# Contexts' way through the second block as a program of its own beside x's, all products 256 wide

## What is computed

```python
def first_block(x, ...):                      # two layers, on x only
    for l in range(DEPTH):
        mix = even_mixer(...) if l % 2 == 0 else odd_mixer(...)   # attention and a recurrence; dilated attention
        x = layer_norm(ALPHA * x + mix, ln1_g[l], ln1_b[l])
        hdn = jnp.square(jax.nn.relu(x @ ffn_w1[l]))              # 1024 -> 4096
        x = layer_norm(ALPHA * x + hdn @ ffn_w2[l], ln2_g[l], ln2_b[l])
        x = x + jax.nn.sigmoid(x @ ple_w_gate[l]) * rms_norm(p[l] @ ple_w_proj[l], ple_norm_g[l])
```

## Time and profile before

| what | us |
|---|---|
| three timed runs, median (lowest to highest) | 1990.55 (1989.61 to 1991.17) |
| the profiled execution, device time | 1993.38 |
| its span in the profile | 1992.1 |
| TensorE busy in the span | 1874.0 |
| VectorE busy | 1096.3 |
| ScalarE busy | 885.6 |

### The profile page before, as it was taken

One profiled execution on the slowest core, in us unless ns is written; L12 is line 12 of the kernel. 1 busy time (PEld: TensorE's weight loads), 2 busy tenths in 40 slices (PEclk: granted clock), 3 DMA queues, 4 the chain that ended last, 5 costly groups with the idle time before them and its releaser, 6 DMA issues. The chain is left out here.

```text
span 1992.1 us, 29858 instructions
## 1 busy us (share of the span) xinstructions
PE 1874.0 (94%) x12320; PEld 1583.5 (79%) x12320; DVE 1096.3 (55%) x1971; ACT 885.6 (44%) x1495; POOL 94.2 (5%) x92
## 2 busy tenths in 40 slices
PE   6988999999999999889999989999999799979998
PEld 5956899978868999677775668888888687569998
DVE  5556656566756565646546663333334575555554
ACT  4554545355435453655434442222232664444443
POOL 0000100040001000310101000000000001100000
PEclk9989999999999999898999989999999899989999
DMA  7477655575366555331220022222322222124553
GB/s 267 162 250 267 218 184 184 191 263 202 104 236 230 185 181 183 131 111 46 75 85 22 23 73 95 99 94 94 104 96 96 74 75 85 53 85 161 185 184 107
DMA packets 79624, 276.88 MB, mean 139 GB/s; under 512 B 9200, under 2 KB 13168, under 8 KB 79488
## 3 DMA queue, kind: packets, MB, share of 16 engines
q1 hardware_dynamic: 77840, 269.66, 39.9%
q0 software_dynamic: 1648, 5.31, 0.9%
HBM read 273.88 MB, written 1.05 MB: 138 GB/s over the span
## 5 line engine op out<-in xcount | busy, mean ns | idle before, releaser
L404 DVE TENSOR_TENSOR low<-ring,high 128x1024 fp32r<-128x1024 f32 x410 | 502.4, 1227 | 436.2 <-ACT high L396 434.9
L429 PE MATMUL bank<-XH,high 128*128 128x256 f32 (+1 forms) x2096 | 684.4, 327 | 60.8 <-DVE XL L1511 21.8
L430 PE MATMUL bank<-XL,high 128*128 128x256 f32 (+1 forms) x2096 | 666.0, 318 | 0.0
L431 PE MATMUL bank<-XH,low 128*128 128x256 f32 (+1 forms) x2096 | 665.1, 317 | 0.0
L396 ACT CAST high<-ring 128x1024 fp32r<-128x1024 f32 x410 | 428.1, 1045 | 471.8 <-PE bank L431 418.8
L429 PEld LDWEIGHTS bank<-XH,high 128*128 128x128 f32 x2096 | 406.5, 194 | 117.0 <-DVE XL L1511 27.4
L430 PEld LDWEIGHTS bank<-XL,high 128*128 128x128 f32 x2096 | 407.7, 195 | 23.8 <-issue 0.2
L431 PEld LDWEIGHTS bank<-XH,low 128*128 128x128 f32 x2096 | 407.0, 194 | 24.6
L431 PE MATMUL bank<-hidden_high,low 128*128 128x256 f32 (+1 forms) x864 | 264.6, 306 | 0.0
L430 PE MATMUL bank<-hidden_low,high 128*128 128x256 f32 (+1 forms) x864 | 264.1, 306 | 0.0
L429 PE MATMUL bank<-hidden_high,high 128*128 128x256 f32 (+1 forms) x864 | 261.9, 303 | 0.0
(11 more groups left out here) (304 smaller groups left out, 1934.4 us busy)
## 6 DMA issues: line engine op xcount, KB each, us to landing
ring<-in_stream SPq DMA_DIRECT2D x410, 512.0 KB, 3.2
ring_mod<-in_stream SPq DMA_DIRECT2D x96, 512.0 KB, 5.5
nb<-in_rpb POOLq DMA_DIRECT2D x12, 256.0 KB, 3.2
X<-in_x SPq DMA_DIRECT2D x2, 512.0 KB, 4.0
X<-in_ctx SPq DMA_DIRECT2D x1, 1024.0 KB, 7.4
out<-y SPq DMA_DIRECT2D x8, 128.0 KB, 2.0
pT<-in_p POOLq DMA_DIRECT2D x2, 256.0 KB, 6.3
c_window<-in_window POOLq DMA_DIRECT2D x1, 512.0 KB, 4.3
```

Source lines behind the costliest of these rows:

```text
L404: nc.vector.tensor_tensor(k.low[:, j % SPLIT, :], k.ring[:, j % RING, :], k.high[:, j % SPLIT, :].bitcast(F32), ALU.subtract).then_inc(*V. ...
L429: nc.tensor.matmul(out, wh, xh, start=(i == 0), stop=False)
L430: nc.tensor.matmul(out, wh, xl, start=False, stop=False)
L431: m = nc.tensor.matmul(out, wl, xh, start=False, stop=(c == ks[-1]))
```

## The change

Contexts get a program of their own. `Path("x")` and `Path("c")` each have their own `X`, `XH`, `XL`, squares, roots, temporaries, small rows and slots of banks, and each takes its weights from its own `Stream`. x's is the 410 tiles as before. Contexts' is a second one, `side`, of 110 tiles: 97 for layer 0 and 13 for layer 1's keys, values and states. They are read a second time from where x's copy of them lies in HBM (`TILE_AT`), with two raw slots and two cast slots, and are cast and split anew. Every product with weights stationary is now 256 wide.

Beside that: `low` now shares its memory with the raw ring (five slots, three for `high`), so that a raw slot is free only when TensorE has used the tile, not when VectorE has split it. Banks are 0 and 1 for x's products, 5 to 7 for x's small steps (with 0 and 1 where needed), and 2 to 4 for everything of contexts and the modulations. Attention has two slots of scores instead of three. The swiglu is done in three parts of the width instead of two, and its silu is made from tanh with two steps on VectorE. The function tables of ScalarE are tracked, which gives 30 table loads instead of 43. The copy of x on GpSimd at the end of each first-block layer is gone.

Order is set by a pace: a part of class `Pace` has a rank that depends on how many tiles it has used against a plan over the planner's clock. The modulations' plan is all 96 tiles by 300 us of that clock. Contexts' plan begins at 300 and is 17 tiles by 850 and 110 by 1520. Behind its plan a part has rank -3 (modulations) or -6 (contexts) and goes before everything else; ahead of it, 3 and 5. Contexts start only when all modulations are done.

```diff
-RING = 4
-SPLIT = 4
+RING, SPLIT = 5, 3
+RING_SIDE, SPLIT_SIDE = 2, 2
 RING_MOD = 4
+MAIN_TILES, MOD_TILES = 410, 96
...
+        self.main = Stream(self, "main", RING, SPLIT, None)
+        self.side = Stream(self, "side", RING_SIDE, SPLIT_SIDE, second_tiles("c", 0) + second_tiles("c", 1))
...
-        self.banks = {"gemm": Slots(self, (0, 1)), "bg": Slots(self, (2,)), "small": Slots(self, (3, 4, 5, 6, 7))}
-        self.tmp, self.sq = Slots(self, (0, 1, 2, 3)), Slots(self, (0, 1))
-        self.stream = {"main": [], "mod": []}
-        self.order, self.blocks, self.expected = [], [], {}
+        state = {}
+        x.gemm, x.banks, x.wide = (Slots(self, ids, state) for ids in ((0, 1), (5, 6, 7), (5, 6, 7, 0, 1)))
+        c.gemm = c.banks = c.wide = Slots(self, (2, 3, 4), state)
...
+def tensor_contexts(k):
+
+
+    yield "mod", 1, MOD_PASSES - 1
+    for layer in range(DEPTH):
+        yield from tensor_second(k, k.pc, layer)
...
+def sync_tiles(k, st):
 
     nc, D_ = k.nc, k.D
-    for j in range(k.n_tiles["main"]):
-        if j >= RING:
-            D_.wait_ge(k.s_low_, (yield "low", j - RING))
+    n = MAIN_TILES if st.plan is None else len(st.plan)
+    if st is k.side:
+
+        D_.wait_for((yield "mod used", MOD_TILES - 1))
+    for j in range(n):
+        if j >= st.n_ring:
+            D_.wait_for((yield st.name, "used", j - st.n_ring))
         else:
             yield None
-        nc.sync.dma_start(k.ring[:, j % RING, :], k.io["stream"][len(k.order)]).then_inc(
-            *D_.tick(k.s_raw[j % RING], 0.1, ("raw", j), by=16, later=3.3))
+        at = j if st.plan is None else TILE_AT[st.plan[j]]
+        nc.sync.dma_start(st.ring[:, j % st.n_ring, :], k.io["stream"][at]).then_inc(
+            *D_.tick(st.s_raw[j % st.n_ring], 0.1, (st.name, "raw", j), by=16, later=3.3))
         D_.clock += 1.3
...
+    for j in range(MAIN_TILES if st.plan is None else len(st.plan)):
+        if j >= st.n_split:
+            A.wait_for((yield st.name, "used", j - st.n_split))
+        A.wait_ge(st.s_raw[j % st.n_ring], (yield st.name, "raw", j))
+        nc.scalar.copy(st.high[:, j % st.n_split, :], st.ring[:, j % st.n_ring, :]).then_inc(
+            *A.tick(st.s_high, A_us(TB * P), (st.name, "high", j)))
...
+def vector_low(k, st):
...
+        V.wait_ge(st.s_high, (yield st.name, "high", j))
+        nc.vector.tensor_tensor(st.low[:, j % st.n_ring, :], st.ring[:, j % st.n_ring, :],
+                                st.high[:, j % st.n_split, :].bitcast(F32), ALU.subtract).then_inc(
+            *V.tick(st.s_low, V_us(TB * P), (st.name, "low", j)))
...
+        nc.scalar.activation(w.TMP[:, j, :], k.bank[k.bank_of[tag, "gate", "product", i]][:, 0:SEQ], ACT.Tanh,
+                             scale=0.5).then_inc(*A.tick(k.s_copied, A_us(SEQ), (tag, "tanh", i)))
...
+        t = w.TMP[:, k.tmp_of[tag, i], :]
+        nc.vector.scalar_tensor_tensor(t, t, 1.0, k.bank[k.bank_of[tag, "gate", "product", i]][:, 0:SEQ], ALU.add,
+                                       ALU.mult).then_inc(*V.tick(k.s_vec, V_us(SEQ), (tag, "silu", i)))
...
+        nc.vector.scalar_tensor_tensor(t, t, 0.5, k.bank[k.bank_of[tag, "up", "product", i]][:, 0:SEQ], ALU.mult,
+                                       ALU.mult).then_inc(*V.tick(k.s_vec, V_us(SEQ), (tag, "made", i)))
...
+        now, due = self.k.T.clock, 0.0
+        for (t0, n0), (t1, n1) in zip(self.plan, self.plan[1:]):
+            if now >= t0:
+                due = n0 + (n1 - n0) * min(1.0, (now - t0) / (t1 - t0))
+        return self.late if self.done() < due else self.rank
+
+
+MOD_PLAN = [(0, 0), (300, MOD_TILES)]
+SIDE_PLAN = [(300, 0), (850, 17), (1520, 110)]
...
+    mods = Pace(k, lambda: len(k.mod_blocks) / TB, MOD_PLAN, -3, 3)
+    side = Pace(k, lambda: len(k.side.blocks) / TB, SIDE_PLAN, -6, 5)
+    k.add(T, tensor_modulations(k), mods)
+    k.add(T, tensor_contexts(k), side + 1)
+    k.add(A, scalar_high(k, k.main), split_ahead(k, k.main, -1, 2))
+    k.add(V, vector_low(k, k.main), split_ahead(k, k.main, -1, 2))
+    k.add(A, scalar_high(k, k.side), side)
```

More of the change, by code:

```diff
@@ L1635, in tensor_gla @@
+        for part in range(NQ):
+            T.wait_ge(k.s_copied, (yield ("gla V", w.name, layer), "copied", part))
         T.wait_ge(k.s_act, (yield tag(i), "k turned"))
-        order = list(range(n_chunks)) if d == 0 else [3, 2, 1, 0, 7, 6, 5, 4]
+        order = gla_order(d)
+        steps = order if w.name == "c" else order[:-1]
         banks = []
         for j in range(2):
-            banks.append((yield from k.banks["small"].take(T, (tag(i), "state", n_chunks - 2))))
+            banks.append((yield from w.banks.take(T, (tag(i), "state", len(steps) - 1))))
@@ L2264, in emit @@
+    k.add(V, vector_final(k, x), 0)
     k.add(D_, sync_stores(k), 0)
     k.run()
-    for which, j in k.order:
-        k.blocks += k.stream[which][j * TB:(j + 1) * TB]
-    k.split = k.n_tiles["main"]
-def vector_gains_all(k, jobs):
-    for layer, name, section, tag, after in jobs:
-        for x in after:
-            if isinstance(x, tuple):
-                k.V.wait_for((yield x))
-        first = section // DC
-        yield from vector_gains(k, layer, name, section, tag, range(first, first + 2))
```

1801 lines of the change are left out of this document (952 added, 849 removed).

## The result

The changed kernel took 1997.69 us (median of 9 runs, 1993.22 to 2007.63), the kernel before 1989.61 us (9 runs, 1984.61 to 1992.23). The ratio is 1.0055, 95% interval 1.0037 to 1.0074: **8 us slower** by the medians (11 by the ratio), where 1.6% faster was forecast. The profiled execution took 1999.76 us, with a span of 1998.5.

The account below looks back on a forecast made before the run. TensorE, busy 94%, was taken as the bound. 1993.4 + 31.5 - 70 + 8 + 3 - 4 = 1961.9; with timed runs 2.8 us lower, 1959 us, 1.6% faster. Own range 1942 to 1978; 8 in 10, 1915 to 2015.

Parts of the forecast that it names:

- splitting: Second block's layer 0: 2352 products 512 wide become pairs of 256, each pair 0.0134 us more on TensorE: +31.5 us.
- the start: All 96 modulation tiles come before about main tile 91, leaving early transfers no slack: +8 us, between 0 and +20.
- fewer buffers: x's attention with two score slots, small steps with three banks, and a shorter cast lead: +3 us, 0 to +12.
- filling and layer 1: Side products fill TensorE's gaps, -70 us (bounds -115 and -20); second block's layer 1, -4 us.
- 95 us of loss: TensorE's loss from 400 to 1525 us, taken as the middle of the two bounds; three quarters was to be filled.
- lower bound of 69: Middle stretch's loss as idle time of 46.6 us plus the clock's shortfall of 22.5 us.
- upper of 120: Middle stretch's loss with eight gaps lost end to end (85.9), 11.3 us idle outside them and 22.5 of clock.
- 25 or less as the sign of filling: Idle plus slow clock between main tile 91 and x's layer 1 was to fall from 69 to 25 us or less.
- A second stream at no cost: 110 more tiles fetched, cast and split would make neither VectorE (66%) nor ScalarE the bound: costed at nothing.
- the side tiles come late: Rival: x's products wait behind uncast side tiles, 2018 us, chance 0.22; sign: such waits over 35 us in sum.
- Layer 1: Second block's last stretch: x's recurrence chain is shorter but loses context products as cover: -4 us, -15 to +10.
- Cancel: Rival: two fifths of the loss are filled, so the gain and the split's cost cancel: 1991 us, chance 0.08.

Follow-up runs that it names:

- e2: Kernel before, with every 512-wide product with weights stationary issued as two of 256, each with its own weight load: 2020.8 us, ratio 1.0149.
- e3: Kernel before, with the modulations on the changed kernel's early plan (all 96 tiles by 300 us of the planner's clock): 2013.0 us, ratio 1.0118.
- e4: Kernel before, with the changed kernel's ring: low parts in the raw ring's memory, five raw slots held until used, three high slots: 1982.6 us, ratio 0.9963.
- e5: Changed kernel, with the modulations back in the places they have in the kernel before and contexts' start moved behind them: 1982.9 us, ratio 0.9968.
- c4: c2 with contexts' parts on TensorE held while ahead of their plan, so that they do not fill: 1997.9 us, ratio 1.0041.
- c2: e11 with c1's edit to the pace of contexts' remaining steps: 1981.4 us, ratio 0.9958.
- e8: Changed kernel, with contexts' plan drawn out so that 19 side tiles are left for x's second layer: 2037.6 us, ratio 1.0235.
- c1: Changed kernel, with contexts' remaining steps keeping a late part's rank once all 110 side tiles are used: 1991.4 us, ratio 1.0023.
- e11: e5 with the rope products of x's second layer allowed any of five banks instead of three small ones: 1977.7 us, ratio 0.9949.
- e6: Changed kernel, with seven of the eight tiles of each modulation sum multiplied over 32 columns instead of 256, modulations computed only in part: 1986.2 us.

## Why the prediction was wrong, step by step

| term | forecast | what the runs say |
|---|---|---|
| splitting | +31.5 | +29.6, alone (e2) |
| the start | +8 | +23.5, alone, all modulations early (e3) |
| fewer buffers | +3 | the ring -7.4, alone (e4); slots of scores and banks not tried alone |
| filling and layer 1 | -74 | -38: what is left of +8.1 |
| sum | -31.5 | +8.1 |

The remainder takes the parts as additive, which no run proves, and it is -35 where the sum is taken by the ratio (+10.9). The largest miss is the filling, 36 us short; the start is 15.5 us over its term, and the ring gave back 10.

**Splitting** was right, by the pace of the windows. Two details were not: 168 of the 2352 products lie in layer 1 (56 blocks there, 552 and 176 in layer 0), and the formula quoted beside it gives 2.5 ns a pair.

**The start was the step that failed first.** I asked only what the transfers of the early tiles would do and called their products "little TensorE work (768 records in all)". They cost 0.66 us each up to the next product, 0.76 with the one after, where they stand alone between products. I had counted records and not looked at what the next product did. In the first stretch idle time did not grow, so the transfers that I had feared are at most a small part (e5, with 31 tiles fewer there, has 5 us less of idle time); e3 shows that the move alone costs 23.5 us in the kernel before; e5 that undoing it in the changed kernel gives 15 back.

**Filling was the second.** Its sum took 95 us of loss in a stretch whose filled parts already had a filler. Idle time from tile 100 to 313 was 53.7 us and the low clock, by the rows, (1 - 0.97) x 466 + (1 - 0.98) x 694 = 28 us, 82 in all, for nearly the same stretch nearer to my lower bound of 69 than to my upper of 120 (which also counted the low clock inside gaps that it took as lost whole). After, they are 27 idle and 16, 43 in all, where I had named 25 or less as the sign of filling. Some 38 us went, the size of the table's remainder, where I took three quarters of 95. The small products in the gaps, which made my upper bound, are still there to be done. Of the 27 us of idle time that are left, 11 are waits for casts of side tiles, the largest item; the rest is small waits, and why the clock's 16 us are left is open. And the side tiles did not come to empty gaps: in the first block they took in part the place of the modulations, which had to go somewhere, as the gap at ln1 of its layer 1 shows. That filling works at all is shown by c4: without half of the filler it is 16.5 us slower than c2.

**A second stream at no cost** was nearly right: stationary-weight products wait 10.1 us in sum for side casts, and the values another 0.7,

```profile
PE bank L548 <- DVE low_side L523: 10.1, 6, 4.4
```

all of it from tile 100 to 313, and part in gaps that would be idle anyway. That is under the 35 us that I had set for the rival "the side tiles come late", so this rival did not happen either, though e8 shows that it can: with 19 tiles left for a stage that needs them it cost 40 us.

**Layer 1** gained nothing: it is 28.2 us shorter, where 13 tiles of context products had left. By the paces of the earlier trace rows these are 34 us there, since 168 products went from 512 to 256 wide (18 us) and half of the products that make the values went altogether (16 us); its clock fell from 0.96 to 0.93. A pace that counts tiles gave contexts' last recurrence a filler's rank, and x waited for it at a low clock (c1, 7 us); x's ropes stood behind its recurrence for want of banks (e11, 7 us); together they gain no more than one of them (c2).

None of the rivals was the outcome. "Cancel" came near, 1991 us, and its filling of 38 us is just what the table leaves; what it lacked is the cost of the start. It gave no reason for so small a filling, so this is mostly luck.

## What to carry to other kernels

Before new work is put in gaps, list what fills them now and where that will go: a filler that is moved between products costs its full pace, which is read from the start of the product ahead of it to the start of the second one behind it, and not from its count of records. Nor is a filler free in a gap once other work could fill it (e5). A pace for a side program should count to its last step, not to its last tile, where the main program waits for that step. Of a loss, count idle time and low clock, not the length of the gap.

## What the runs showed that was not expected

Eight records with a stationary operand 32 wide cost 0.76 us in a stream of 256-wide products (0.66 up to the next one), and 0.38 (0.28 to 0.29) when their rows are 32 instead of 256 wide; right behind such a group a second one adds 0.43 us. Thinning this filler dropped the mean clock of a gap from 0.96 to 0.77 with the same count of records (e6). Two products of 256 in place of one of 512 cost 0.2387 us against 0.2252, and in e2's stream, where two neighbours of every three have the same high weights, 419 products still fill 50 us: none of them is quicker for it than where the weights differ.
